# Shorter norms, a router input made during the last output products, reordered loads and an eleventh early expert slab

## What is computed

```python
h = h + rms_norm(merged @ w_out[i], norm_post_mix[i])
v = rms_norm(h, norm_pre_mlp[i])
ff = jnp.square(jax.nn.relu(v @ w_up[i])) @ w_down[i]
h = h + rms_norm(ff, norm_post_mlp[i])
e = (p[i] @ w_ple[i]) * jax.nn.sigmoid(h @ w_ple_gate[i])
h = h + rms_norm(e, norm_ple[i])
...
mixed = jax.nn.sigmoid(ga) * (o_a @ w_proj_a) + jax.nn.sigmoid(gb) * (o_b @ w_proj_b)
x = x + mixed @ w_out
x = x + hier_moe(rms_norm_2(x, g_ffn), w_group, b_group, w_expert, b_expert, w1, w3, w2)
```

## Time and profile before

| | us |
|---|---|
| median of 3 runs (lowest to highest) | 1471.92 (1468.37 to 1473.09) |
| the profiled execution's own time | 1471.43 |
| its span, first to last instruction | 1469.6 |
| PE busy | 1201.3 (82% of the span) |
| DVE busy | 433.0 (29%) |
| ACT busy | 241.2 (16%) |
| POOL busy | 144.4 (10%) |
| DMA, mean over the span | 225 GB/s, 330.66 MB |
| mean granted TensorE clock | 0.921 of full |

### The profile page before, as it was taken

The page is one execution under the profiler, slowest core; times in us unless marked ns, Lnnn a source line. Parts: engine busy times, 40 slices in busy tenths (PEclk is TensorE's granted clock), DMA queues, the critical chain, the costliest instruction groups (busy, mean ns, idle before and its releaser), DMA issues. The chain is left out here.

```text
span 1469.6 us, 13840 instructions
## 1 busy us (share of the span) xinstructions
PE 1201.3 (82%) x5905; PEld 680.3 (46%) x5905; DVE 433.0 (29%) x761; ACT 241.2 (16%) x470; POOL 144.4 (10%) x168
## 2 busy tenths in 40 slices
PE   7999999999993999999879999887564664646645
PEld 6846655556841899444434446445221221212211
DVE  1142333035513554644764362213000000000002
ACT  1131002136500222001211156001000000000001
POOL 1001003000210224430132100100000000000000
PEclk9999999999997999999999999997887887978868
DMA  9533132441006444343334210692999999999994
GB/s 367 193 144 115 66 112 109 179 165 58 1 0 279 186 173 164 136 181 149 115 129 171 86 58 30 249 383 111 431 428 427 429 426 427 427 428 428 428 426 185
DMA packets 26980, 330.66 MB, mean 225 GB/s; under 512 B 4112, under 2 KB 4896, under 8 KB 6176
## 3 DMA queue, kind: packets, MB, share of 16 engines
q1 hardware_dynamic: 26912, 329.70, 55.7%
HBM read 328.64 MB, written 1.05 MB: 224 GB/s over the span
## 5 line engine op out<-in xcount | busy, mean ns | idle before, releaser
L226 PE MATMUL ps<-ring,arena 128*128 128x512 f32 (+2 forms) x2008 | 732.5, 621 | 116.2 <-DMA arena<-in_w 65.1
L226 PE MATMUL ps<-arena 128*128 128x128 f32 (+10 forms) x2356 | 484.5, 422 | 79.1 <-DMA misc<-in_w 32.6
L226 PEld LDWEIGHTS ps<-ring,arena 128*128 128x128 f32 (+2 forms) x2008 | 278.9, 164 | 469.5 <-issue 463.8
L226 PEld LDWEIGHTS ps<-arena 128*128 128x128 f32 (+3 forms) x2356 | 257.9, 171 | 209.5 <-issue 177.5
L226 PE MATMUL ps<-arena,ring 128*128 128x128 f32 (+1 forms) x768 | 116.1, 313 | 1.4 <-DVE arena L293 1.4
L1813 DVE TENSOR_TENSOR arena<-ps,arena 128x512 f32<-128x512 f32 x8 | 5.5, 692 | 372.3 <-PE ps L226 372.3
L229 PE MATMUL ps<-cst,arena 128*128 128x128 f32 x472 | 68.5, 291 | 56.5 <-POOL arena L324 30.3
L226 PEld LDWEIGHTS ps<-arena,ring 128*128 128x128 f32 x768 | 107.9, 193 | 9.4 <-issue 2.3
L229 PEld LDWEIGHTS ps<-cst,arena 128*128 128x128 f32 x472 | 56.7, 150 | 80.0 <-POOL arena L324 33.5
L226 PE MATMUL ps<-misc,arena 128*32 128x512 f32 (+3 forms) x232 | 88.1, 540 | 0.0
L375 DVE TENSOR_TENSOR arena<-ring 128x1024 f32<-128x1024 f32 (+1 forms) x15 | 27.7, 1849 | 74.8 <-PE ps L226 43.5
(11 more groups left out here) (253 smaller groups left out, 637.4 us busy)
## 6 DMA issues: line engine op xcount, KB each, us to landing
ring<-in_w SPq DMA_DIRECT2D x45, 2048.0 KB, 29.5
arena<-in_w SPq DMA_DIRECT2D x38, 2048.0 KB, 30.0
ring<-in_w_in SPq DMA_DIRECT2D x27, 2048.0 KB, 7.8
misc<-in_w SPq DMA_DIRECT2D x9, 2048.0 KB, 31.4
ring<-in_w_up SPq DMA_DIRECT2D x8, 2048.0 KB, 10.0
ring<-in_w_down SPq DMA_DIRECT2D x8, 2048.0 KB, 7.8
ring<-in_w_out SPq DMA_DIRECT2D x4, 2048.0 KB, 11.3
ring<-in_w SPq DMA_DIRECT2D x5, 1024.0 KB, 21.3
```

The lines of the kernel that those rows point to most:

```text
L226: return lambda q: q.matmul(out_, l, r, start=s, stop=e, skip_group_check=skip)
```

## The change

1. `norm_half`: the 1/D goes into the squares' scale, the sum and EPS are one instruction, the products with the gain row run beside the squares (for data in PSUM after each square), and one 128x1024 instruction on DVE multiplies by 1/sqrt and adds to `X`. POOL has no part. For the MLP's result the row factors `column(10 + m)`, `column(12 + m)` are made earlier.
2. The slabs of `w_up` 0 and 1 go to SP ahead of `w_ple`, `norm_post_mlp` and `w_in_2_idx`. `rest_of_up` is called one product earlier, with the two `ple_part` of it first. After the MLP `down_products(6, (7, 4))` and the norm stand ahead of `ple_part`.
3. The three projection jobs of layer 2 get their PSUM units by name.
4. `OO[0]` is turned ahead of the last attention product, `OO[1]` after the first `w_proj_a_2` step; the first half of `M2T` is made within `w_proj_b_2`, the second within tile 0 of `w_out_2`.
5. Router: the gain goes into the router's weights (one DVE instruction on 128x288), `X` is turned in quarters, with turn, squares, 1/sqrt and router product of half 0 within tile 1; the expert logits stand ahead of the group logits, so that one instruction per half scales both.
6. An eleventh slot at U(3, 2) takes `w2_2` of expert 2 early; the buffers of `fours` that were double (XE, PG, GPT, YS, GH, HT) become single. `up` waits for its two gathered halves apart, and `combine(k - 1)` goes ahead of `gates(k)`.

```diff
-        def norm_half(m, part, dst, row, t_row, rs=None):
+        def norm_half(m, part, dst, row, t_row, rs=None, in_psum=False):
...
+            v, y, x, sq, pr = column(6 + 2 * m), column(m), column(4 + m), [], []
             for j, (cs, P, t) in enumerate(part):
...
+                sc = D ** -0.5 if rs is None else column(rs[0] + m)
+                ta = act.op(lambda q, P=P, j=j, w=cs.stop - cs.start, sc=sc: q.activation(junk[:, 0:w], P, ACT.Square, scale=sc, accum_out=column(6 + 2 * m + j)),
                             t, act.now(), dve.now() if (m, j) == (0, 0) else None)
...
+                sq.append(ta)
+                pr.append(dve.op(lambda q, P=P, cs=cs: q.tensor_tensor(dst[:, m, cs], P, row[:, cs], ALU.mult), ta if in_psum else t, t_row))
+            t = dve.op(lambda q: q.tensor_scalar(v, v, column(7 + 2 * m), EPS, ALU.add, ALU.add), ta)
             t = rsqrt1(v, y, x, t)
             if rs is not None:
-                t = dve.op(lambda q: q.tensor_tensor(y, y, r2, ALU.mult), t)
...
-            for cs, P, _ in part:
-                a = dve.op(lambda q, P=P, cs=cs: q.scalar_tensor_tensor(dst[:, m, cs], P, y, row[:, cs], ALU.mult, ALU.mult), t, t_row)
-                h = (cs.start + cs.stop) // 2
-                for eng, c2 in ((pool, slice(cs.start, h)), (dve, slice(h, cs.stop))):
-                    res.append(eng.op(lambda q, c2=c2: q.tensor_tensor(X[:, m, c2], X[:, m, c2], dst[:, m, c2], ALU.add), a))
-            return res
+                t = dve.op(lambda q: q.tensor_tensor(y, y, column(rs[1] + m), ALU.mult), t)
+            return dve.op(lambda q: q.scalar_tensor_tensor(X[:, m, :], dst[:, m, :], y, X[:, m, :], ALU.mult, ALU.add), t, pr), sq + pr
...
+        job = next_job([A["w_up"][0], A["w_up"][1]], {n: [att_over, pe_ybt] for n in (4, 5, 6)})
         t_ple = sp.dma(U(7), A["w_ple"], s_ple, 16, pe.now())
...
-        job = next_job([A["w_up"][0], A["w_up"][1]], {n: [att_over, pe_ybt] for n in (4, 5, 6)})
...
-            tmp_free = seven(job, S, tmp, tmp_free, False, put, nxt, hooks)
+            tmp_free = seven(job, S, tmp, tmp_free, False, put, nxt, hooks, [(ub, uc), (ua, ud), (ub, uc)][i])
...
+        slab_users[NR + 5] = t_ot
+        take("w2_2", 2, NR + 5)
...
-        parts = [tiled(m, turn_half(GA2, M2T, None, m, mg_t[m])) for m in range(2)]
...
+        part = tiled(0, m2t[0], (None, lambda: m2t.append(turn_half(GA2, M2T, None, 1, mg_t[1]))))
+        add_in(0, part)
...
+        part = tiled(1, m2t[1], (first_turned, lambda: routed.append(route(0))))
+        t_rs = [row_rs(0)]
         pe_out = pe.now()
+        add_in(1, part)
...
+        for j in range(2):
+            turn_quarter(1, j)
+        square(1, 0)
+        square(1, 1)
+        routed.append(route(1))
+        t_rs.append(row_rs(1))
...
-            XE = [U(2, 0.5, j * 1024).rearrange("p (c s) -> p c s", c=8) for j in range(2)]
-            YS = [U(3, 0.5, j * 1024) for j in range(2)]
+            XE = U(1, 0.5).rearrange("p (c s) -> p c s", c=8)
...
+            YS, GH = U(2, 0.5), U(2)[:, 1024:1536]
```

More of the change, by code:

```diff
@@ L400, in pair_job, with seven @@
             return {"B": B, "tok": tok, "ops": ops, "k": (k0, k1), "free": free}
-        def seven(job, S, tmp, tmp_free, turned, put, nxt, hooks={}):
+        def seven(job, S, tmp, tmp_free, turned, put, nxt, hooks={}, units=None):
             B, tok = job["B"], job["tok"]
-            (PB, ib), (PA, ia) = unit(), unit()
+            (PB, ib), (PA, ia) = (unit(), unit()) if units is None else [(PS[i], i) for i in units]
             kept.add(ia)
@@ L1326, in y_part @@
         def y_part(m):
-            return [(slice(n * 512, n * 512 + 512), YC[:, m, n * 512:n * 512 + 512], [y[str(m + 1) + str(n + 1)], t_rs[m]]) for n in range(2)]
+            return [(slice(n * 512, n * 512 + 512), YC[:, m, n * 512:n * 512 + 512], [y[str(m + 1) + str(n + 1)], t_r2]) for n in range(2)]
         YN = U(4).rearrange("p (m n) -> p m n", m=2)
@@ L1589, in build, with turn_out @@
                         mask, PT2, fin2(w), tT[qn], tT[kn], tV[vn], t_dm if w else t_cm, pe.now()))
[L1590 to L1593 removed]
         OT = [U(7, 0.5).rearrange("p (c t) -> p c t", c=4), U(7, 0.5, 1024).rearrange("p (c t) -> p c t", c=4)]
         ot = []
[L1596 removed]
+        def turn_out(w):
             P, i = unit()
@@ new lines, in square, with row_rs @@
+        def square(m, j):
+            squared[m] = act.op(lambda q: q.activation(junk[:, 0:512], X[:, m, j * 512:j * 512 + 512], ACT.Square, scale=D ** -0.5,
+                                                  accum_out=column(6 + 2 * m + j)), t_h[m][j], act.now())
+        def row_rs(m):
+            v = column(6 + 2 * m)
+            t = dve.op(lambda q: q.tensor_scalar(v, v, column(7 + 2 * m), EPS, ALU.add, ALU.add), squared[m])
+            return rsqrt1(v, column(SC4 + m), column(4 + m), t)
@@ new lines, in build, with turn_quarter @@
+        PT_, ti = unit()
+        kept.add(ti)
+        def turn_quarter(m, j):
+            B = PT_[:, j * 512:j * 512 + 512]
+            t = pe.group([tr(B[:, c * 128:c * 128 + 128], X[:, m, (4 * j + c) * 128:(4 * j + c) * 128 + 128]) for c in range(4)],
+                         t_h[m][j], t_t.get((m - 1, j)), unit_users[ti] if m == 0 else None)
+            o = XT[:, 4 * j:4 * j + 4, m * 128:m * 128 + 128]
+            pv = B.rearrange("p (c t) -> p c t", c=4)
+            if j:
+                t_t[m, j] = dve.op(lambda q: q.tensor_copy(o, pv), t)
+            else:
+                t_t[m, j] = act.op(lambda q: q.activation(o, pv, ACT.Copy), t)
@@ new lines, in route, with first_turned @@
+        def route(m):
+            for j in range(2):
+                t = pe.group([mm(PR_[:, m * 512:m * 512 + 36], XT[:, c, m * 128:m * 128 + 128], rw[:, c, :], c == 0, c == 7)
+                              for c in range(4 * j, 4 * j + 4)], t_t[m, j], t_rw, unit_users[ri] if m == 0 else None)
+            return t
+        part = tiled(0, m2t[0], (None, lambda: m2t.append(turn_half(GA2, M2T, None, 1, mg_t[1]))))
+        add_in(0, part)
+        PR_, ri = unit()
+        kept.add(ri)
+        def first_turned():
+            for j in range(2):
+                turn_quarter(0, j)
+            for j in range(2):
+                square(0, j)
@@ L1862, in combine @@
                     cbn[n] = cb[k]
-            order[:] = [early[x][2] for x in [("w1_2", e) for e in range(4)] + [("w3_2", e) for e in range(4)] + [("w2_2", e) for e in range(2)]]
+            order[:] = [early[x][2] for x in [("w1_2", e) for e in range(4)] + [("w3_2", e) for e in range(4)] + [("w2_2", e) for e in range(3)]]
             choose(0)
@@ L2037, in next_way @@
             at.update(held[3])
+            spilled = early.pop(("w2_2", 2), None)
+            if spilled:
+                for q_ in (act, dve):
+                    q_.wait(spilled[1])
         fours()
```

194 lines of the change are left out of this document (96 added, 98 removed).

## The result

The change took 1418.08 us, median of 4 runs (1417.67 to 1421.63), beside 1471.01 for the kernel before in the same session (1468.37 to 1473.09): a ratio of 0.9646, 95% interval 0.9624 to 0.9669. The forecast was 1414.6, from 1410 to 1424. The time is inside the range, 3.5 us above the forecast. The profiled execution took 1418.26 with a span of 1416.5, 53.1 less than the 1469.6 of before; the sum had 56.8.

What follows compares the result with a forecast made beforehand. PE bounds the kernel until the first expert slot comes free at 1022.04, then DMA at 427 GB/s. Five terms sum to 56.8 us: span 1469.6 to 1412.8, plus 1.8 gives 1414.6; range 1410 to 1420, 1424 with the first rival.

Steps and rivals of the forecast that it cites:

- Term 1: After the mix: PE's 23.0 us wait for the first norm half goes, plus 2.9 us of clock; 25.9 us.
- Term 2: Later norm halves after MLP and gate: waits of 3.51, 1.00 and most of 2.81 go, slow rows quicken; 9.3 us.
- Term 3: Second projection job: named PSUM units remove the 7.44 us wait, but POOL's RoPE limits the gain; 0.8 us, between 0 and 1.9.
- Term 4: From attention to the router: tile 1 of `w_out_2` ends 5.4 us earlier, the stretch behind it gives 10.5; 15.9 us.
- Term 5: Expert stream: the eleventh early slab takes one of 86 slabs out of the DMA stream; 4.9 us.
- Slab in the way: At `w_out_2`: slower slabs make its load late and PE waits, up to 4.9 us, 1415 to 1419.5; chance 0.13.
- Load not early: After the mix: SP's list holds the early `w_up` load until 440.5, gain there about 6, time 1434; chance 0.05.
- Starved: Expert phase: single buffers free slots late and stop the DMA each round, 63 us, time 1478; chance 0.02.
- Clock: About `w_out_2` or the jobs: PE keeps half its clock, 2 to 4 us lost, inside the range; no separate chance.

Runs made afterwards that it cites:

- after: The first profiled execution of the full change, against the kernel before: 1418.26 us, span 1416.5.

## Why the prediction was right, and what its sum got wrong

The distances from before to the profiled execution of the change, stretch by stretch, add up to the 53.1 us of the span:

| stretch | before | after | gain | predicted |
|---|---|---|---|---|
| to B | 418.15 | 419.96 | -1.8 | 0 |
| B to the last of the later norm halves (729.47, 696.68) | 311.32 | 276.72 | 34.6 | 25.9 + 7.8 |
| to the last product of the jobs (819.18, 785.36) | 89.71 | 88.68 | 1.0 | 1.5 + 0.8 |
| to `w_proj_a_2` (921.92, 885.88) | 102.74 | 100.52 | 2.2 | 2.8 |
| to the first free slot (1022.04, 972.62) | 100.12 | 86.74 | 13.4 | 13.1 |
| to the last down product (1449.18, 1394.24) | 427.14 | 421.62 | 5.5 | 4.9 |
| to the end | 20.42 | 22.26 | -1.8 | 0 |

**Term 1, 25.9.** Right in size and cause: 26.1 up to the first later norm half with the order of two large and three small loads alone, 23.8 when that order is taken back in the change. It is half of the whole gain.

**Term 2, 9.3.** Right in its cause, and about a microsecond too large. Up to the last of the later norm halves the change is 7.1 us ahead of the kernel with only the loads moved (276.7 and 283.9 from B), where I had 7.8; up to the last product of the jobs it is 8.4, and by the old norms put back 7.8 of that is the norm's length with the clock behind it. What no run bears out is that each wait brings its own slow rows. I had taken 1.4 us of them behind the wait of 3.51 for the norm's; with only the loads moved the wait stood and they were gone.

**Term 3, 0.8.** The step that failed by most of its size, though small: 0.0, the lower end that I gave, "DVE and POOL hold the pace". I had read from the kernel before that L1422 ends at 765.6, and taken part of the way to it as a gain; the wait simply moves behind the product, and named units against units in turn measure 0.1 us apart. The 1.0 us of this stretch is what term 2 has behind the last norm half, 1.4, less 0.4 that job 3 loses. That the row of 3.31 us on POOL is itself 2 us too long I had before me and did not ask about.

**Term 4, 15.9.** 2.2 + 13.4 = 15.6. Right in the sum and in its places: the end of tile 1 to the logits (984.99 to 998.97 before, 946.15 to 951.09 after) gave 9.0 where I had 8.9, and the logits to the free slot 1.5 where I had 1.6. Not right in its reason: I wrote of the half router product inside tile 1 as though it earned something, and the experiment with it outside shows nothing. In six of the profiled executions, the change's two among them, a stretch of PE at less than the full clock also appears between 820 and 870 (granted 0.88 and 0.95 in `after`), which the kernel before doesn't show. The stretch to `w_proj_a_2` takes 100.5 us in those six and 99.3 in the other four of the changed kernels; so it cost 1.2, and without it the stretch would have given 3.5 instead of 2.2.

**Term 5, 4.9.** 5.5, and 5.4 by taking it away. The slot was free no later, so the margin of 1.3 us for `w_out_2` was enough.

**What no term had.** 1.8 us are ahead of B, and chance of the execution, since the change's second profiled execution has B 4.1 earlier; the clock windows up to 410 show 1.7 more lost here than in the kernel before. In that second execution the span was 1411.9, 0.9 under the sum. The other 1.8 are at the end and not chance: every profiled execution with the changed expert phase takes 7.1 to 8.2 us from the issue of the last store to the end, the two with the old one 5.6 and 5.7. The stretch from the last data to the end, in `after` and in the kernel with only the loads moved, by the same query:

```profile
1410.00:1413.00 3.00, 0.00 (x0) 0.00 (x0) 0.19 (x1) 0.00 (x0) 0.00 (x0) 0.50 0.83 330
1413.00:1416.50 3.50, 0.00 (x0) 0.00 (x0) 0.00 (x0) 0.00 (x0) 0.00 (x0) 0.50 0.01 4
```

```profile
1440.00:1441.30 1.30, 0.00 (x0) 0.00 (x0) 0.00 (x0) 0.00 (x0) 0.00 (x0) 0.50 0.00 0
```

The data are moved as fast as before; then 3.5 us pass with nothing on any engine, 1.3 to 1.6 in the kernels with the old expert phase. What the program does there the trace doesn't show. It isn't the waits that the change adds for the eleventh slab on the other ways through the experts: the kernel with ten slabs has none of them and ends the same way, 3.3 us after its data. The cause stays open.

**The rivals.** *Slab in the way:* PE never waited for `w_out_2`. By the prediction's estimate, the Trainium skill's 358 GB/s ("SBUF — State Buffer", section "A bandwidth-pool intuition that's wrong (but worth ruling out)") would have made it late; the stream held 427 to 428 in this trace, as it had before. *Load not early:* the slabs were issued at 369.23 and at 419.95 less the 1.8. *Starved:* no slice under 424 from slice 28 to the last but one. *Clock:* a loss did come, 1.7 us ahead of B and 1.2 at 830 to 850, not where I had named it. For the router's rows the trace agrees with the row taken and not with the Trainium skill's issue floor ("TensorE: Matmul & The Clock Gate", section "Back-to-back issue gap"): 16 rows of 128x36 took 1.87 and 2.03 us, 0.12 to 0.13 each, as the row of 128x72 had. The same section says of the formula behind that floor that it has no budget for weight loads, which each of these matmuls has.

## What to carry to other kernels

Look for a long wait in the list of loads before looking at the code it delays: two loads issued ahead of three small ones gave 26 us, the rewritten norm at its four later places 6 to 8. When you take a wait away, follow the same chain one link further: here the named units only moved 7.4 us from one side of a product to the other, and the link behind it, an addition that took 3.31 us where its like takes 1.27 and the sums around it, was worth 10 us. And measure the parts of a change one by one, from a place ahead of them to the next place that all kernels share: the most intricate of them, the router inside the output product, was worth nothing here.

## What was unexpected

DVE and POOL stop each other. A 128x512 addition on POOL takes 1.26 us alone and 3.25 to 3.31 beside DVE's 128x2048 sum, and the sum 2.98 to 3.36 instead of 2.28. In job 2 of the change POOL's addition is recorded from 728.17 and ends at 731.48, 1.1 us after DVE's sum has ended at 730.37: by these times it does not run slowly, it stands and then runs. Three more pairs shown above read the same way: POOL's addition ends 1.1 us after the sum that ends at 430.59, at 729.80 and at 733.08, a little less than its own 1.26. That agrees with the Trainium skill ("SBUF — State Buffer", section "Who interferes with whom"), by which the two share one pair of ports to SBUF as an exclusive lock. The same pair costs nothing where both are off the path: the 3.24 and 3.24 us at 428 to 434 above.

An execution can lose 1.7 to 6.9 us of clock in its first 410 us, in unchanged code. One and the same kernel ran from 1413.7 to 1423.5; whether such losses are all of that spread isn't shown, since only one execution of each run has a trace. Nor does a wait of a given length bring a given loss: behind 3.51 us PE ran at a granted clock of 0.50 in the kernel before and at 1.00 with the loads moved. Medians of five runs left the named units open by 1.5 us, where the distance between two rows of the trace settled them to 0.1.
